# Attention values of two branches issued alternately in opposite column halves, one branch one head later, with the division and the rests of the outputs moved to GpSimd

## What is computed

```python
def causal_softmax_attention(q, k, v):          # per head, keys of 96, values of 64
    w = softmax(where(mask, q @ k.T * scale, -inf))
    return w @ v

def stick_breaking_attention(q, k, v):          # per head, keys and values of 64
    z = q @ k.T * scale
    log_1m = where(mask, log_sigmoid(-z), 0)
    suffix = cumsum(log_1m, reverse=True) - log_1m
    return where(mask, exp(log_sigmoid(z) + suffix), 0) @ v

o_mla, o_sb = ...                                # 512 tokens x 512 each
merged = sigmoid(gate_mla) * (o_mla @ w_branch_mla) + sigmoid(gate_sb) * (o_sb @ w_branch_sb)
h = h + merged @ w_out
```

## Time and profile before

| what | value |
|---|---|
| time, median of 3 runs | 2427.37 us (2427.21 to 2428.22) |
| the profiled execution: its time | 2424.88 us |
| its span, first to last instruction | 2423.6 us |
| mean granted TensorE clock | 0.976 of 2.4 GHz |
| busy: PE, DVE, ACT, POOL | 97%, 35%, 19%, 53% of the span |
| attention heads (first stick logits to first matmul of the merge) | 1770.15 to 1901.79 us of the span |

### The profile page before, as it was taken

How to read it: one execution, slowest core, us unless ns; L and a number is a source line. 1 busy time by engine, 2 the same in 40 slices (tenths; PEclk the granted TensorE clock), 3 DMA queues, 4 the chain that set the end, 5 groups by cost and what they waited for, 6 DMA issues and landing times.

```text
span 2423.6 us, 26205 instructions
## 1 busy us (share of the span) xinstructions
PE 2349.8 (97%) x11108; PEld 1938.4 (80%) x11108; DVE 839.4 (35%) x910; ACT 448.4 (19%) x712; POOL 1287.7 (53%) x734
## 2 busy tenths in 40 slices
PE   7999999999989999999999999999899999999999
PEld 6888888787768888888888888778667788888887
DVE  2323103666444333203232202430568733333013
ACT  2111003222313111003111102011257221111012
POOL 4666665754015666665666665666100456666654
PEclk9999999999679999999999999999899999999999
DMA  4333332221002333332333332233100222333322
GB/s 155 97 99 100 96 96 78 81 76 61 9 27 87 96 96 96 96 97 77 96 97 100 99 96 80 87 96 98 35 1 1 62 91 92 96 96 96 106 87 86
DMA packets 55580, 201.06 MB, mean 83 GB/s; under 512 B 6408, under 2 KB 6536, under 8 KB 55336
## 3 DMA queue, kind: packets, MB, share of 16 engines
q1 hardware_dynamic: 53712, 193.62, 25.8%
q10 hardware_dynamic: 1752, 5.77, 0.6%
HBM read 197.27 MB, written 2.10 MB: 82 GB/s over the span
## 4 chain that ended last, share of the span: by engine, by line
PE 69%; DVE 4%; ACT 1%; issue 1%; POOL 0%; DMA 0%; DVEq 0%; POOLq 0%; ACTq 0%
PE psum L340 13%; PE psum L341 13%; PE psum L342 13%; PE psum L402 6%; PE psum L400 6%; PE psum L401 6%; PE psum L478 2%; PE psum L813 1%; PE psum L821 1%; PE psum L850 1%; PE psum L592 1%; PE psum L438 1%; PE psum L959 1%; PE psum L960 1%; PE psum L961 1%
## 5 line engine op out<-in xcount | busy, mean ns | idle before, releaser
L322 POOL TENSOR_SCALAR w_hi<-w_raw 128x1024 fp32r<-128x1024 f32 (+1 forms) x365 | 396.6, 1087 | 1089.0 <-PE psum L342 583.6
L324 POOL TENSOR_TENSOR w_lo<-w_raw,w_hi 128x1024 fp32r<-128x1024 f32 (+1 forms) x365 | 891.7, 2443 | 30.5
L340 PE MATMUL psum<-u_hi,w_hi 128*128 128x512 f32 (+1 forms) x2072 | 791.3, 382 | 11.1 <-DVE work L1527 4.0
L341 PE MATMUL psum<-u_hi,w_lo 128*128 128x512 f32 (+1 forms) x2072 | 787.5, 380 | 0.0
L342 PE MATMUL psum<-u_lo,w_hi 128*128 128x512 f32 (+1 forms) x2072 | 787.0, 380 | 0.0
L340 PEld LDWEIGHTS psum<-u_hi,w_hi 128*128 128x128 f32 x2072 | 390.7, 189 | 87.9 <-DVE work L1527 4.5
L342 PEld LDWEIGHTS psum<-u_lo,w_hi 128*128 128x128 f32 x2072 | 390.7, 189 | 74.2
L341 PEld LDWEIGHTS psum<-u_hi,w_lo 128*128 128x128 f32 x2072 | 390.7, 189 | 73.1 <-issue 0.5
L400 PE MATMUL psum<-w_hi,hidden_hi 128*128 128x512 f32 x768 | 298.8, 389 | 0.0
L401 PE MATMUL psum<-w_lo,hidden_hi 128*128 128x512 f32 x768 | 298.8, 389 | 0.0
L402 PE MATMUL psum<-w_hi,hidden_lo 128*128 128x512 f32 x768 | 298.8, 389 | 0.0
(11 more groups left out here) (261 smaller groups left out, 1776.7 us busy)
## 6 DMA issues: line engine op xcount, KB each, us to landing
w_raw<-in_ffn_in SPq DMA_DIRECT2D x176, 512.0 KB, 3.5
w_raw<-in_ffn_out SPq DMA_DIRECT2D x88, 512.0 KB, 3.5
w_raw<-in_proj_in SPq DMA_DIRECT2D x34, 512.0 KB, 3.5
w_raw<-in_mix_in SPq DMA_DIRECT2D x29, 512.0 KB, 3.4
w_raw<-in_embed SPq DMA_DIRECT2D x10, 512.0 KB, 3.5
w_raw<-in_mix_out SPq DMA_DIRECT2D x8, 512.0 KB, 3.5
w_raw<-in_branch SPq DMA_DIRECT2D x8, 512.0 KB, 3.6
w_raw<-in_proj_out SPq DMA_DIRECT2D x8, 512.0 KB, 3.5
```

The source lines that it names most:

```text
L322: pool.tensor_scalar(hi, raw, 1.0, 1.0, ALU.mult, ALU.mult).then_inc(k.w_split, 1)
L324: pool.tensor_tensor(lo, raw, hi.bitcast(F32), ALU.subtract).then_inc(k.w_split, 1)
L340: pe.matmul(out, hi[:, cols], xhi, start=first, stop=False)
L341: pe.matmul(out, lo[:, cols], xhi, start=False, stop=False)
```

## The change

- The two value products of a pass are issued as one list, a matmul of the stick branch and one of the softmax branch in turn (`values(h, m)`). The softmax branch is one head behind (m = h-1), so the two write opposite halves of their banks' partitions, which are opposite column halves of TensorE's array. The last pass is followed by the softmax branch's head 7 alone.
- The turned probabilities get a second buffer for odd heads, in two pieces (`turned_at`).
- The four multiplications of the division move from VectorE to GpSimd (`pool_attend`), and so do the rests of the output tiles, but for the last two (`last_pairs`).
- VectorE copies the softmax branch's values out (`mla_out`) directly behind `stick_out` and ahead of `softplus`; before, it came behind `softplus`.
- `maxima` starts after the first of the four logit blocks instead of after all.
- The merge takes tiles 4 to 7 before tiles 0 to 3; the order in which the tiles are completed is new (`COMPLETE`).

```diff
--- before.py
+++ after.py
@@ -180,7 +180,7 @@
         self.hid_hi, self.hid_lo = sem("hid_hi"), sem("hid_lo")
 
         self.proj_scaled = sem("proj_scaled")
-        self.pair_hi, self.pair_lo = sem("pair_hi"), sem("pair_lo")
+        self.pair_hi, self.pair_lo, self.last_lo = sem("pair_hi"), sem("pair_lo"), sem("last_lo")
 
         self.qf_taken, self.filled, self.gates_taken = sem("qf_taken"), sem("filled"), sem("gates_taken")
         self.lb_step, self.lb_exp, self.k_done, self.logf_done = sem("lb_step"), sem("lb_exp"), sem("k_done"), sem("logf_done")
@@ -324,11 +324,30 @@
     pool.tensor_tensor(lo, raw, hi.bitcast(F32), ALU.subtract).then_inc(k.w_split, 1)
 
 
+def pool_attend(k):
+
+    pool, H = k.nc.gpsimd, Heads(k)
+
+    def pairs(h):
+        for n in COMPLETE.get(h, ()):
+            pool.wait_ge(k.pair_hi, KD + PAIRS.index(n) + 1)
+            pool.tensor_tensor(tile(k.ulo, n), H.o[n], tile(k.uhi, n).bitcast(F32), ALU.subtract).then_inc(k.pair_lo, 1)
+
+    for h in range(AH):
+        pool.wait_ge(k.rs_inv, h + 1)
+        for i, c in ROWS:
+            w = H.probs[:, c:c + (i + 1) * P]
+            d = pool.tensor_scalar(w, w, H.rs[:, h * NT + i:h * NT + i + 1], None, ALU.mult)
+        d.then_inc(k.divided, 1)
+        pairs(h)
+
+
 def gpsimd_program(k):
     pool = k.nc.gpsimd
     spare = NUMBER["branch", 0] + 1
     for n in range(len(CHUNKS)):
         if n == spare:
+            pool_attend(k)
 
             pool.wait_ge(k.soft_summed, AH)
         pool_split(k, n)
@@ -779,7 +798,9 @@
         self.K = [tile(k.uf, KD + h) for h in range(AH)]
         self.v, self.sv = k.B(0), k.big[:, 14 * T:18 * T]
         self.sq, self.sk = [tile(k.big, 6 + n) for n in range(4)], [tile(k.big, 10 + n) for n in range(4)]
-        self.probs, self.turned, *self.z = (row(k.big[:, (KF + LATENT_AT) * T:], n) for n in range(4))
+        self.probs, turned, *self.z = (row(k.big[:, (KF + LATENT_AT) * T:], n) for n in range(4))
+
+        self.turned = [[(0, N_CAUSAL, turned)], [(0, 2 * T, k.big[:, 4 * T:6 * T]), (2 * T, N_CAUSAL, k.diag[:, 0:N_CAUSAL - 2 * T])]]
         self.soft = [row(k.scf, n) for n in range(2)]
         free = NUMBER["branch", 0] % PAIR
         self.soft_hi, self.soft_lo = k.split_sums[(free + 1) % PAIR][:, :], k.split_sums[(free + 2) % PAIR][:, :]
@@ -793,10 +814,14 @@
 
         self.o = self.sk + self.sq
 
-
-
-COMPLETE = {1: [0], 3: [1], 4: [4], 5: [2, 5], 6: [6], 7: [3, 7]}
+    def turned_at(self, h, c, n):
+        return next(x[:, c - a:c - a + n] for a, b, x in self.turned[h % 2] if a <= c and c + n <= b)
+
+
+
+COMPLETE = {3: [0], 4: [4], 5: [1, 5], 6: [6], 7: [2], 8: [7, 3]}
 PAIRS = [n for h in sorted(COMPLETE) for n in COMPLETE[h]]
+CAUSAL_BLOCKS = sorted(CAUSAL, key=lambda x: (x[0], x[1]))
 
 
 def pe_attend(k):
@@ -849,7 +874,8 @@
             n = (i + 1) * P
             pe.matmul(k.psum[:, c:c + n], H.Q[h][0:QK, i * P:(i + 1) * P], H.K[h][0:QK, 0:n], start=True, stop=True)
             m = pe.matmul(k.psum[:, c + n - P:c + n], H.id16, H.ngt16, start=False, stop=True, skip_group_check=True)
-        m.then_inc(k.logits_done, 1)
+            if i in (ROWS[0][0], ROWS[-1][0]):
+                m.then_inc(k.logits_done, 1)
 
     def transpose(h):
         pe.wait_ge(k.divided, h + 1)
@@ -860,21 +886,30 @@
                 m = pe.transpose(k.psum[:, to:to + P], H.probs[:, c + j * P:c + (j + 1) * P], k.cst(C_ID))
         m.then_inc(k.p_turned, 1)
 
-    def stick_values(h):
-        pe.wait_ge(k.z_weights, h + 1)
-        if h:
-            pe.wait_ge(k.z_out, h)
-        v_at = lambda i: H.sv[:, ((h // 2) * NT + i) * P + h % 2 * HV:((h // 2) * NT + i) * P + (h % 2 + 1) * HV]
-        pe_causal_values(pe, k.ps[7][half(h), :], v_at, H.z[h % 2]).then_inc(k.z_values, 1)
-
-    def mla_values(h):
-        pe.wait_ge(k.p_copied, h + 1)
-        if h:
-            pe.wait_ge(k.o_out, h)
-        else:
-            pe.wait_ge(k.norm_var, NORM["heads"])
-        v_at = lambda i: H.v[:, (h * NT + i) * HV:(h * NT + i + 1) * HV]
-        pe_causal_values(pe, k.ps[6][half(h), :], v_at, H.turned).then_inc(k.o_values, 1)
+    def values(h, m):
+
+        if h is not None:
+            pe.wait_ge(k.z_weights, h + 1)
+            if h:
+                pe.wait_ge(k.z_out, h)
+        if m is not None:
+            pe.wait_ge(k.p_copied, m + 1)
+            if m:
+                pe.wait_ge(k.o_out, m)
+            else:
+                pe.wait_ge(k.norm_var, NORM["heads"])
+        last = len(CAUSAL_BLOCKS) - 1
+        for n, (i, t0, width, c) in enumerate(CAUSAL_BLOCKS):
+            if h is not None:
+                v = H.sv[:, ((h // 2) * NT + i) * P + h % 2 * HV:((h // 2) * NT + i) * P + (h % 2 + 1) * HV]
+                z = pe.matmul(k.ps[7][half(h), t0:t0 + width], v, H.z[h % 2][:, c:c + width], start=n == 0, stop=n == last, skip_group_check=True)
+            if m is not None:
+                v = H.v[:, (m * NT + i) * HV:(m * NT + i + 1) * HV]
+                o = pe.matmul(k.ps[6][half(m), t0:t0 + width], v, H.turned_at(m, c, width), start=n == 0, stop=n == last, skip_group_check=True)
+        if h is not None:
+            z.then_inc(k.z_values, 1)
+        if m is not None:
+            o.then_inc(k.o_values, 1)
 
     def spread_key(h):
         if h >= 2:
@@ -892,15 +927,14 @@
         logits(h)
         if h:
             transpose(h - 1)
-            stick_values(h - 1)
-            mla_values(h - 1)
+            values(h - 1, h - 2 if h > 1 else None)
         else:
             for n in range(2, AH):
                 spread_key(n)
     stick_sums(AH - 1)
     transpose(AH - 1)
-    stick_values(AH - 1)
-    mla_values(AH - 1)
+    values(AH - 1, AH - 2)
+    values(None, AH - 1)
 
 
 def pe_merge(k):
@@ -913,12 +947,15 @@
             pe.wait_ge(k.merge_dve, 3 * (j - 2) + 2)
         else:
             pe.wait_ge(k.probs_done, AH)
-        for part in range(2):
+        for part in (1, 0):
             for t in range(4):
                 kk = 4 * part + t
                 if j == 0:
                     pe.wait_ge(k.pair_hi, KD + PAIRS.index(kk) + 1)
-                    pe.wait_ge(k.pair_lo, KD + PAIRS.index(kk) + 1)
+                    if kk in COMPLETE[AH]:
+                        pe.wait_ge(k.last_lo, COMPLETE[AH].index(kk) + 1)
+                    else:
+                        pe.wait_ge(k.pair_lo, KD + PAIRS.index(kk) + 1)
                 m = mm3(pe, k.ps[b + part], hi, lo, slice(kk * P, (kk + 1) * P), tile(k.uhi, kk), tile(k.ulo, kk), t == 0, t == 3)
         m.then_inc(k.w_used, 1)
 
@@ -1339,8 +1376,10 @@
 
     def pairs(h):
         for n in COMPLETE.get(h, ()):
-            act.wait_ge(k.o_out, h + 1)
-            act.wait_ge(k.z_out, h + 1)
+            if n < 4:
+                act.wait_ge(k.o_out, 2 * n + 2)
+            else:
+                act.wait_ge(k.z_out, 2 * n - 6)
             act.copy(tile(k.uhi, n), H.o[n]).then_inc(k.pair_hi, 1)
 
     act.preload_act_table_set("natural_log_exp_and_others")
@@ -1356,9 +1395,9 @@
         if h:
             act.wait_ge(k.soft_summed, h)
         act.copy(H.soft_hi, s).then_inc(k.soft_hi, 1)
-        pairs(h - 1)
+        pairs(h)
     weigh(AH - 1)
-    pairs(AH - 1)
+    pairs(AH)
 
 
 def act_embed(k):
@@ -1913,8 +1952,10 @@
         dve.tensor_tensor(zh, zh, k.psum[:, B0:B0 + N_CAUSAL], ALU.add).then_inc(k.z_added, 1)
 
     def maxima(h):
-        dve.wait_ge(k.logits_done, h + 1)
-        for i, c in ROWS:
+        dve.wait_ge(k.logits_done, 2 * h + 1)
+        for n, (i, c) in enumerate(ROWS):
+            if n == 1:
+                dve.wait_ge(k.logits_done, 2 * h + 2)
             x = h * NT + i
             d = dve.tensor_reduce(H.mx[:, x:x + 1], k.psum[:, c:c + (i + 1) * P], AX.X, ALU.max)
         d.then_inc(k.row_max, 1)
@@ -1924,9 +1965,11 @@
 
     def turned(h):
         dve.wait_ge(k.p_turned, h + 1)
-        if h:
-            dve.wait_ge(k.o_values, h)
-        dve.tensor_copy(H.turned, k.psum[:, B0:B0 + N_CAUSAL]).then_inc(k.p_copied, 1)
+        if h >= 2:
+            dve.wait_ge(k.o_values, h - 1)
+        for a, b, x in H.turned[h % 2]:
+            d = dve.tensor_copy(x[:, 0:b - a], k.psum[:, B0 + a:B0 + b])
+        d.then_inc(k.p_copied, 1)
 
     def stick_out(h):
         dve.wait_ge(k.z_values, h + 1)
@@ -1951,16 +1994,11 @@
         hs = slice(h * NT, (h + 1) * NT)
         dve.wait_ge(k.probs_done, h + 1)
         dve.reciprocal(H.rs[:, hs], H.rs[:, hs]).then_inc(k.rs_inv, 1)
-        dve.wait_ge(k.rs_inv, h + 1)
-        for i, c in ROWS:
-            w = H.probs[:, c:c + (i + 1) * P]
-            d = dve.tensor_scalar(w, w, H.rs[:, h * NT + i:h * NT + i + 1], None, ALU.mult)
-        d.then_inc(k.divided, 1)
-
-    def pairs(h):
-        for n in COMPLETE.get(h, ()):
+
+    def last_pairs():
+        for n in COMPLETE[AH]:
             dve.wait_ge(k.pair_hi, KD + PAIRS.index(n) + 1)
```

(12 more changed lines are left out.)

## The result

The changed kernel takes 2444.42 us in the median against 2427.29 before, ratio 1.0078 (95% interval 1.0061 to 1.0095): 17 us slower, and in the spans of the profiled executions 2442.9 against 2423.6, 19.3 longer. The direction was forecast; the size was 2434.3 and the range ended at 2441.

| stretch | before | after | difference | forecast |
|---|---|---|---|---|
| span's start to first stick logits | 1770.15 | 1770.75 | +0.6 | 0 |
| to the first transposition | 31.29 | 30.79 | -0.5 | -0.6 |
| six passes, to the seventh transposition | 81.87 | 96.88 | +15.0 | +4.2 |
| to the eighth | 12.79 | 15.49 | +2.7 | +1.2 |
| to the merge | 5.69 | 7.47 | +1.8 | +2.1 |

A forecast was written before the change was run, and what follows sets the result against it. TensorE's 13.65 us a pass and a 13.44 us ring through the other engines bound it nearly equally. Head 0 -0.6, first pass -0.2, five passes +4.4, last pass +1.2, end +2.1 gave +6.9: 2434.3 us, range 2429.5 to 2441.

The forecast's parts named there:

- the fourth rival: TensorE's clock in the passes: busy some 80%, it stays at 2.4 GHz; nothing added, no chance given.
- the sum: All terms over head 0, the passes and the end: together +6.9 us, time 2434.3.
- The ring: Pass-to-pass chain: stick copy-out, VectorE's softplus, ScalarE's rounded part, TensorE's sums, logits, transposition, values; 13.44 us, after the change 14.53.
- The joint values: Both branches' value matmuls in opposite column halves: 2.67 us, bounds 2.33 (full overlap) and 4.67 (none).
- my 0.33: Stick values end at 2.67 instead of 2.34 us, so their copy-out starts 0.33 later in each pass.
- its cover: Time from GpSimd's division start until the transposition needs it: 3.4 to 3.9 us, hiding a division taken as 1.9.
- The copy's place: Softmax copy ahead of the softplus on VectorE enters the ring: 0.72 us a pass, bounds 0.61 and 0.83.
- Head 0, the first pass, the end: Head 0 -0.6 from earlier maxima; first pass 13.44 for 13.65, -0.2; head 7 alone before the merge +2.1.
- The port that both engines share: VectorE and GpSimd blocking each other during the division: taken as 0; meeting the softplus, up to 2 us in the ring.
- no overlap: Rival: column halves of the joint values don't overlap, ring 16.4 us, +20, time 2448; chance 0.13.
- the sign of being wrong: Pass length afterwards: under 13.6 us means the ring was not tight, over 15.5 no overlap or a late division.
- Faster, the ring isn't the bound: Rival: the stick copy waits in VectorE's own queue; passes fall to about 11.7 us, time about 2417; chance 0.09.

The follow-up runs named there:

- The added work: The changed kernel with 16 added matmuls of 256 columns, read by nobody, ahead of the suffix sums in every pass but the first: 2433.5 us, ratio 1.0034.
- its sister: The changed kernel with the same 16 added matmuls and the division back on VectorE, softmax copy still ahead of the softplus: 2438.4 us, ratio 1.0045.

## Why the prediction was wrong, by its own steps

- **The step that failed** is the fourth rival: "TensorE will be busy some 80% of a pass. In the last pass it was busy 2.35 of 4 us and the granted clock stayed 1.00 ... I add nothing." It took one pass, which a full one precedes and the merge follows, for a row of like passes. The added work gives its size: 10.3 of the 15.0 us of the six passes, and 1.9 more lie behind them. The rest of the 19.3, some 7 us, is what the sum gave for everything else (6.9). The price was within reach of the trace, whose head 0 had the lower level: sums of 2.8 us at 2.4 GHz become some 2 us longer at 1.2, 14 for seven passes.
- **The ring** was right: bare 13.44 read, 13.42 to 13.59 measured; with the copy 14.15 to 14.25; with all at full clock 14.53 forecast, 14.47 to 14.65 measured. This total was met by two wrong terms that cancel. The joint values took 2.38 to the end and put the copy-out at 2.41, so that my 0.33 was 0: the overlap is full. And the division, taken as 1.9 us in bounds of 1.3 to 2.8, took 4.26, over its cover of 3.4 to 3.9: 0.35 a pass. The upper bound came from a rounding with constants; a multiplication by a column of factors was not among the rows. The estimate of 2.95 us from the Trainium skill's 2.38 times for three column tiles (TensorE: Matmul & The Clock Gate, § Part 3) was too high for these two halves: 2.38 us.
- **The copy's place** at 0.72 was right (0.73 and 0.61 in the timeline after, 0.61 and 0.83 in the ring).
- **Head 0, the first pass, the end**: -0.5 for -0.6 and +1.8 for +2.1. The first pass, forecast at 13.44, took 14.79, and 13.42 with the clock held by 11 added matmuls: the other 1.4 are the clock. The last pass, forecast at +1.2, came to +0.85 and 1.85 for the clock.
- **The port that both engines share** cost nothing in the changed kernel, as forecast: softplus and rest kept 1.47 and 1.49. They did not meet the division: the rest ended at 1826.28, and GpSimd began at 1826.47. Where VectorE's division met two rests on GpSimd it took 3.12 for 1.27. The Trainium skill (Advanced Engine Details and Errata, § VectorE Performance Modes) has such instructions block each other, and these rows agree.
- **The rivals**: "no overlap", whose time of 2448 was nearest, is false in its cause, and so was the sign of being wrong, passes over 15.5 for "no overlap, or the division late": they came, and it was neither. "Faster, the ring isn't the bound" is false, and the kernel with the softplus first shows what it would have taken.

Open: what decides in which pass the clock falls. Work in the gap removed the fall from all six passes of one kernel and not from those of its sister, and gaps of one size went with it and without it.

## What to carry to other kernels

When TensorE looks full, follow the ring through the other engines before counting what a cheaper TensorE step brings: here it was 0.2 us behind TensorE, and each thing put into it counted fully. A gap that opens in TensorE at every turn of a loop can cost twice, once as the gap and once more as a lower clock for what comes after it. Price it at the lower clock before calling it free. Closing it gave the fastest kernel here; filling it held the clock in one kernel and not in another, where the filling itself was slowed and held up the work behind it.

## What was not expected of the hardware

- Float32 matmuls of 64 output columns in opposite column halves overlap completely: 28 records in 2.38 us against 4.67 one after the other, pairs starting within 0.01 us of each other.
- The granted clock fell to 1.2 GHz in every pass of 14.8 to 17.0 us in which TensorE was idle for 1.8 to 2.7 us, and not in the one last pass of before, idle for 3.69 of 12.79. In the kernel before with its copy first, 1.9 to 2.0 us a pass were enough. But with the softplus first and the division on VectorE five of six passes, idle for 1.2 to 2.2 us, kept 1.00; of the six of the kernel before with the softplus first, each idle for 2.09, three did; and one filled pass with 0.90 lost it.
- GpSimd's multiplication of 512 float32 columns by a column of factors took 1.563 us and of 128 columns 0.602, against 1.086 for 1024 columns times constants.
